# Every third residual of the last stages' weights computed by GpSimd instead of VectorE, in a hybrid decoder step

## The reference

```
mod = silu(c) @ w_ada + b_ada                  # shifts, scales and gates of both halves
h   = rms_norm(x, g_norm1) * (1 + sc1) + sh1
q, k, v, glu_a, glu_b, gate_a, gate_c = split(h @ w_in)
attn = moba_attention(q, k, v, cached pages) @ w_attn_proj
cv   = silu(layer_norm(depthwise_conv(glu))) @ w_conv_proj
x   = x + gt1 * ((sigmoid(gate_a) * attn + sigmoid(gate_c) * cv) @ w_out)
h2  = rms_norm(x, g_norm2) * (1 + sc2) + sh2
f_g, f_u = split(h2 @ w_ffn_in)
x   = x + gt2 * ((silu(f_g) * f_u) @ w_ffn_out)
```

## Time and profile before

| what | value |
|---|---|
| median of three runs | 586.12 us (584.86 to 587.48) |
| span of the profiled execution | 584.0 us (no time of its own is listed beside it) |
| PE busy | 523.6 us, 90% |
| DVE busy | 394.2 us, 67% |
| ACT busy | 292.1 us, 50% |
| POOL busy | 170.0 us, 29% |

### The profile page before, as it was taken

How to read it: one execution, slowest core, us unless ns; L and a number is a source line. 1 busy time by engine, 2 the same in 40 slices (tenths; PEclk the granted TensorE clock), 3 DMA queues, 4 the chain that set the end, 5 groups by cost and what they waited for, 6 DMA issues and landing times.

```text
span 584.0 us, 10410 instructions
## 1 busy us (share of the span) xinstructions
PE 523.6 (90%) x4180; PEld 441.1 (76%) x4180; DVE 394.2 (67%) x602; ACT 292.1 (50%) x519; POOL 170.0 (29%) x232
## 2 busy tenths in 40 slices
PE   3769899988979879798798999899999999999997
PEld 3658678865655646556458888799999999999996
DVE  1742674789999998999765865567565656554441
ACT  3144433587777877655653532293444444434331
POOL 8326377287778776750100000000000000000000
PEclk9589898897999999999979999999999999999999
DMA  8999459698999999999676989946466446476501
GB/s 306 370 369 388 165 189 346 224 357 296 405 399 397 420 401 416 366 366 414 260 296 245 387 291 374 364 148 213 150 221 206 147 158 164 122 192 169 153 20 38
DMA packets 82128, 159.31 MB, mean 273 GB/s; under 512 B 2573, under 2 KB 61113, under 8 KB 76952
## 3 DMA queue, kind: packets, MB, share of 16 engines
q1 hardware_dynamic: 76256, 89.27, 45.8%
q0 software_dynamic: 5120, 67.71, 28.9%
q10 hardware_dynamic: 703, 1.67, 0.8%
HBM read 156.39 MB, written 2.72 MB: 272 GB/s over the span
## 4 chain that ended last, share of the span: by engine, by line
PE 57%; DVE 21%; DMA 10%; issue 5%; ACT 4%; POOL 1%; SPq 1%; ACTq 1%; DVEq 0%; POOLq 0%
PE acc L1580 12%; PE acc L1581 12%; PE acc L1582 12%; DVE prod L1057 7%; DMA wring<-in_w_in 6%; DVE sall L1064 4%; PE acc L1452 3%; DMA wring<-in_w_ffn_in 2%; PE acc L1465 2%; PE acc L1467 2%; PE acc L1466 2%; DMA pr<-in_page_table 2%; PE acc L1384 2%; PE chain L1604 2%; ACT L623 1%
## 5 line engine op out<-in xcount | busy, mean ns | idle before, releaser
L1129 DVE TENSOR_TENSOR wlo<-wring,whi 128x1024 fp32r<-128x1024 f32 (+2 forms) x84 | 92.0, 1097 | 72.2 <-ACT whi L623 71.4
L623 ACT ACTIVATE whi<-wring 128x1024 fp32r<-128x1024 f32 (+2 forms) x84 | 80.1, 958 | 83.2 <-PE acc L1582 77.4
L1580 PE MATMUL acc<-xlo,whi 128*128 128x264 f32 x384 | 110.2, 287 | 3.5 <-DVE wlo L1129 1.3
L1581 PE MATMUL acc<-xhi,wlo 128*128 128x264 f32 x384 | 108.8, 283 | 0.0
L1582 PE MATMUL acc<-xhi,whi 128*128 128x264 f32 x384 | 108.8, 283 | 0.0
L578 POOL TENSOR_TENSOR cvT<-cvT,cprod 128x256 f32<-128x256 f32 x120 | 87.9, 732 | 42.4 <-ACT cprod L623 27.6
L1452 PE MATMUL acc<-hT,wring 128*128 128x264 f32 x336 | 92.1, 418 | 3.7 <-DMA wring<-in_w_in 3.3
L1580 PEld LDWEIGHTS acc<-xlo,whi 128*128 128x128 f32 x384 | 72.3, 188 | 5.8 <-issue 3.1
L1452 PEld LDWEIGHTS acc<-hT,wring 128*128 128x128 f32 x336 | 63.3, 200 | 17.6 <-DMA wring<-in_w_in 3.7
L1064 DVE TENSOR_REDUCE sall<-prod 128x32 f32<-128x2048 f32 x32 | 73.0, 2281 | 0.4
L1581 PEld LDWEIGHTS acc<-xhi,wlo 128*128 128x128 f32 x384 | 72.4, 188 | 0.1
(11 more groups left out here) (316 smaller groups left out, 913.4 us busy)
## 6 DMA issues: line engine op xcount, KB each, us to landing
wring<-in_w_ffn_in SPq DMA_DIRECT2D x22, 1024.0 KB, 7.7
wring<-in_w_ada SPq DMA_DIRECT2D x20, 1024.0 KB, 15.3
wring<-in_w_in SPq DMA_DIRECT2D x12, 1024.0 KB, 11.3
wring<-in_w_ffn_out SPq DMA_DIRECT2D x16, 704.0 KB, 5.6
more<-in_w_out SPq DMA_DIRECT2D x4, 1024.0 KB, 13.7
more<-in_w_ada SPq DMA_DIRECT2D x4, 1024.0 KB, 12.5
wring<-in_w_in SPq DMA_DIRECT2D x6, 512.0 KB
wring<-in_w_in SPq DMA_DIRECT2D x4, 768.0 KB
```

The costliest lines, as they stand in the source:

```text
L623: return nc.scalar.activation(out, in_, f, **kw)
L1129: v.tensor_tensor(wlo[:, place, 0:n, :], w, whi[:, place, 0:n, :].bitcast(F32), ALU.subtract)\
L1580: mm(bank[:, 0:R], whi[:, place, k - k0, :], lo[:, k, :], start=k == 0, stop=False)
L1581: mm(bank[:, 0:R], wlo[:, place, k - k0, :], hi[:, k, :], start=False, stop=False)
```

## The change

From unit 12 on, each unit whose number leaves the remainder 2 when divided by 3 has its rest made by GpSimd: units 14, 17, 20, ... 89, 26 of the 78 rests from unit 14 on (one of 128x512, 25 of 128x1024). GpSimd does them at the end of its list, each after ScalarE's copy of that unit. VectorE skips them. Who waited for a unit's rest now waits for both counts.

```diff
+POOL_UNITS = [u for u in range(12, len(UNITS)) if u % 3 == 2]
+DVE_UNITS = [u for u in range(len(UNITS)) if u not in POOL_UNITS]
...
+        def rests_done(eng, u):
+
+            eng.wait_ge(wlo_ready, sum(1 for x in DVE_UNITS if x <= u))
+            if u >= POOL_UNITS[0]:
+                eng.wait_ge(wlo_by_pool, sum(1 for x in POOL_UNITS if x <= u))
...
                     elif before in LAST_UNIT:
-                        sp.wait_ge(wlo_ready, LAST_UNIT[before] + 1)
+                        rests_done(sp, LAST_UNIT[before])
...
+            for n_unit in POOL_UNITS:
+                w, place, n, _ = unit(n_unit)
+                pool.wait_ge(whi_ready, n_unit + 1)
+                g.tensor_tensor(wlo[:, place, 0:n, :], w, whi[:, place, 0:n, :].bitcast(F32), ALU.subtract)\
+                    .then_inc(wlo_by_pool, 1)
...
             def split_weights(u):
 
-                if u < len(UNITS):
+                if u in DVE_UNITS:
...
                 place, nk = u % UNIT_RING, {"y": FT, "c": CT, "a": AT}.get(name[0], KD)
-                pe.wait_ge(wlo_ready, u + 1)
+                rests_done(pe, u)
...
             for n in first:
-                pe.wait_ge(wlo_ready, n + 1)
+                rests_done(pe, n)
```

More of the change, by code:

```diff
@@ L325, in program @@
         whi_ready, wlo_ready, part_used = sem("whi_ready"), sem("wlo_ready"), sem("part_used")
+        wlo_by_pool = sem("wlo_by_pool")
         xhi_ready, xlo_ready = sem("xhi_ready"), sem("xlo_ready")
```

## The result

The changed kernel takes 588.67 us (median of 20 runs) against 585.56 us before (20 runs). The ratio is 1.0049, with a 95% interval from 1.0027 to 1.007: slower by 2.9 us, between 1.6 and 4.1. The profiled execution's span is 587.7 us, 3.7 us more than before. The first matmul of unit 0 came 0.4 us later than before, with the change not yet in use; behind it the last unit starts 3.25 us late. That second number is the change's own, and the rest of this text is about it.

What follows compares the result with a forecast made beforehand. TensorE alone was taken to set the time from 400 us on. Terms 0.5 + 0.66 + 0.33 = +1.5 us on the 584.0 us span gave 585.5 us; with the median 2.1 us above, 587.6 us, range 585.0 to 589.9 us.

Steps and rivals of the forecast that it cites:

- TensorE's extra waits: One wait more on TensorE at each of 78 units: taken as 0, at most 0.02 us each, 1.6 us.
- Unit 14: `xlo` held by GpSimd's rest, so ap3's bank and unit 12 come 0.54 us late; range -0.6 to +0.6.
- Unit 17: VectorE's sum held by GpSimd's rest, so ap7's bank and unit 16 come 0.66 us late; range 0 to +0.8.
- Units 20, 23, 26: During GpSimd's rest VectorE only reads PSUM or is idle: 0, bounds +-0.2 us.
- Unit 29: At the FFN's start `flo` waits for GpSimd, making the read of f3 late: +0.33 us, range -0.3 to +0.5.
- The other 20: Remaining moved rests, to unit 89: VectorE's idle time makes up for a held `fhi` or `flo`; 0.
- Is a delay swallowed later?: Delay at 328 or 338 us: the issue waits for TensorE, so the 13.62 us transfer moves too.
- VectorE's busy time: Sign in the changed kernel's profile: some 15 to 25 us lower, not 31, as held instructions count as busy.
- The rival that VectorE isn't held: GpSimd's turn comes in gaps, so VectorE isn't held: -0.9 us, 585.2 us; chance 0.21.
- Clearly faster: VectorE, earlier at every bank, closes more TensorE holes; all 4.9 us gone gives 581.2 us; chance 0.06.
- "Clearly slower" in the FFN: VectorE loses 1.45 us per held rest, up to 618 us, or 601 us if PSUM reads are held; chance 0.10.
- "too late": GpSimd's rests come too late for TensorE: +30 us at most; chance 0.02.

Runs made afterwards that it cites:

- the run with the spare rests: Against the kernel before: VectorE makes all rests, GpSimd makes the 26 again into an unused spare tile; units +8.3 us late from unit 30 on.

## Why the prediction was right, and where not

The forecast was 587.6 us, range 585.0 to 589.9; measured were 588.67 us. The mechanism held for what VectorE loses; a term was missing, and that the number fell inside the range was partly luck. The forecast added 1.5 us; the last unit starts 3.25 us late, and the medians differ by 3.1 us. Two things hid this. The forecast stood on the median of three runs, 586.12 us, which lies 0.56 us above that of twenty. And the sum of the upper bounds, +3.7 us, holds 1.6 us for TensorE's extra waits, which cost 0.01 us; without them the bounds end at +2.1 us, 588.2 us, below the 588.67 us measured. Of the signs that the prediction named, units 12 and 16 came as said (0.51 and 1.31 us late, 0.5 and 1.2 forecast), unit 29 did not (3.24 us late, 1.5 forecast). Term by term:

- Unit 14: forecast +0.54 us, with GpSimd first and `xlo` to 328.64 us. Measured +0.49 in the changed kernel, +0.51 alone; `xlo` took 1.52 us. Right.
- Unit 17: forecast +0.66 at unit 16, measured +0.78, and +0.63 alone; the difference is within what unit 16 does by itself. Right.
- Units 20, 23, 26: forecast 0 with a bound of 0.2; the steps there are -0.08 and +0.15 us, and the second (+0.13) is also in the run that moved none of them. Right.
- Unit 29: forecast +0.33, measured +0.61 in the changed kernel, +0.59 alone. This term was mis-sized. The prediction let `flo` wait for GpSimd; but it is the cast ahead of it that waits, and `flo` comes whole behind it, ending 0.62 us after GpSimd (398.78 against 398.16 us) and not 0.29. The Trainium skill, page SBUF — State Buffer, section Who interferes with whom, says that copies and casts too can take the port that VectorE shares with GpSimd; this trace agrees, with 2.04 us against 0.30 us. By it the term would have come out nearer.
- The other 20 (the prediction counted 21) and TensorE's extra waits: forecast 0, measured +0.01 us each. Right. Among the slots that are released later the prediction left out unit 23's, which the last modulation weights take; units 23 and 24 are both 2.61 us late, so it cost nothing.
- "Is a delay swallowed later?": no, as forecast.
- Missing: TensorE's clock. The prediction let unit 16's delay pass on as it is; but TensorE, idle for 2.06 us ahead of it, was granted half clock for 3.4 us, and unit 16 took 1.23 us longer. This term was put at nothing, without a reason. The terms add up to +1.5 us without it and to +3.25 us as measured: 1.2 us the clock, 0.3 us the cast, the rest the small steps. The run with units 14 and 17 alone shows the clock's part apart from the others.
- VectorE's busy time fell by 23.8 us, where 15 to 25 were forecast; GpSimd's rests took up to 3.44 us.
- Two small slips in the working: with its estimate of 2.25 us for 1024 elements the three terms shrink by 0.16, 0.14 and 0.14 us, 0.44 us together and not 0.3; and the rest of 2.99 us is longer by 0.60 us, not quite the 0.73 us that the other still had.

The rival that VectorE isn't held fell with the first two steps. "Clearly faster" fell; its case was real for two rests, 9 and 24, but neither was among those moved. "Clearly slower" in the FFN and "too late" did not happen. Of the 3.25 us lost, 1.2 are the clock's; without them the change would cost some 2.0 us, 0.35%.

## What to carry to other kernels

Work moved from VectorE to GpSimd is not taken off VectorE if it reads SBUF: VectorE's next instruction with two SBUF inputs, or a cast of the kind here, waits for all of it. So ask of each moved instruction what VectorE has to do in the 2.4 us from its start, and who waits for that; move it only where the answer is reads of PSUM or nothing. Of the 26 moves here 20 were free and won nothing, three nearly so, and three cost time, while two others, standing ahead of a read that frees a bank, brought the last unit forward by 1.2 us, too little for the times to show.

And a hole in TensorE's work can have a price beyond its length: two delays that were cheap one by one cost 1.1 to 1.4 us more together, because the clock fell. Read the granted clock behind every hole that a change makes longer.

## What the runs showed of the hardware that was not expected

- A cast of 128x264 with one SBUF input is held by GpSimd's subtraction: 2.04 us instead of 0.30 us. A product of a PSUM and an SBUF input is not: 0.43 us. In the changed kernel eight casts are held, and each ends 0.15 or 0.16 us after GpSimd's instruction; a held sum or subtraction of 128x264 ends 0.29 us after it.
- GpSimd filling a tile (0.88 us, no SBUF input) does not hold VectorE's sums and subtractions (0.43 us beside it). The one cast beside it took 0.41 instead of 0.30 us.
- Which engine comes first was decided by 0.05 and 0.02 us at two places, the same way in the two profiles of the changed kernel.
- TensorE's granted clock fell to 1.2 GHz for 3.4 us in unit 16 after idle times of 1.29 and 2.06 us, in three of three traces with units 14 and 17 moved, and stayed at 2.4 GHz after 0.80 and 1.91 us and after 1.29 and 1.44 us, in one trace each. All of these have 0.5 and 1.15 us of idle time ahead of units 6 and 7 as well. In the run with the spare rests it fell just after a single 1.92 us ahead of unit 12.
